# A two-block transformer with a 32-expert layer: the first and last expert written out, the first one's down weights beside the ring, the routing without GpSimd, and the gate's bias rows moved

## Chip, cores and metric

One NeuronCore of a Trainium2 chip. The metric is the device time of one execution in microseconds (us); the kernel before takes 2494.17 us, the median of three runs (2492.13 to 2497.22).

## What is computed

A sequence of 256 tokens of width 1024, all in fp32, goes through two layers of one kind (feed-forward, a mixing layer, cross attention, feed-forward) and then one layer of a second kind (a recurrence and a gated linear attention), which ends in a mixture of experts. The change lies in this last part:

```python
logits = xt @ w_router + b_router                  # 256 tokens, 32 experts
top_val, top_idx = lax.top_k(logits, 4); gates = softmax(top_val)
# for every expert e and the tokens that chose it:
hdn = xb @ w_up[e] + b_up[e]                       # 1024 -> 2048
gate_h = minimum(hdn[:, :1024], 7.0); up_h = clip(hdn[:, 1024:], -7.0, 7.0)
act = (up_h + 1.0) * gate_h * sigmoid(1.702 * gate_h)
y = (act @ w_down[e] + b_down[e]) * gate           # 1024 -> 1024, summed over the four experts
# then
h = layer_norm_2(DEEPNORM_ALPHA * h + m, ln2_g, ln2_b)
h = h + sigmoid(h @ w_ple_gate + b_ple_gate) * (p @ w_ple)
```

An expert's up weights are 8 MB and its down weights 4 MB; all 32 are read whatever the routing, 384 MB.

## The kernel before, in words

Every engine has its program written out by hand, with semaphores between them. A helper class counts the semaphores, so a wait names an event. SyncE issues all loads. Weights go through a ring of 12 slots of 1 MB (`ring`, slots 0 to 11). In front of the experts only slots 0 to 5 are filled in turn (`load`, L363); 6 to 11 hold split weights and inputs there. For the experts, `load_pair` (L375) fills two slots by one DMA of 2 MB: four pairs `("moe","u",k)` and two pairs `("moe","d",j)` are one expert, the whole ring. The first pair goes to slots 6 and 7. Each DMA waits until both of its slots are given back by TensorE (`used`), and stands in order behind the one before.

In front of the experts come the output projection (L1041), a layer norm over two halves of 128 tokens, t = 0 and 1 (`ln`, tag "A"), and the routing. For each half TensorE transposes the normed rows (`transposes`, L653), ScalarE copies half of the result to `hT` (L1368), VectorE the other (`evac_T`, L1850), and TensorE multiplies by the router weights (L1074, L1076). `best(t)` on VectorE (L2265 to L2273) takes the four highest and marks them in `chosen`. `best(0)` stands in `first_half`, which `ln` calls ahead of VectorE's copy for t = 1. GpSimd computes `h = hn * g + b` of both halves (`residual`, L2474 and L2475). From `chosen` TensorE counts each token's place in its expert (L1117), VectorE reads the largest count (`most`, L2299 to L2301), and every engine branches on it: at most 64 tokens to an expert is `few()`, else `many()`. The runs here take `few()`.

`few()` on TensorE: `expert_biases` multiplies the 32 gates of each token with the down biases (L1133, over 32 rows) and so opens the sums of banks 4 to 7. `gather` (L1157) picks an expert's tokens by a matmul with a selection matrix that VectorE wrote (`select`, L2322). Then a loop over 32 experts: `gate_up` (L1189, 64 matmuls that give back the eight up slots pair by pair), `turned(0)`, the next expert's `gather`, `turned(1)`, `combine("back")` (L1166) that adds the previous expert's result, the gates turned (`GT`), and the down matmuls (L1227). ScalarE copies out, takes the sigmoid (L1753) and copies the down result (L1338). After the loop stands `combine("last")`.

After the branch, VectorE adds the residual (`joined`, L2409) and norms (L2425), TensorE writes the gate's bias into banks 4 to 7 by matmuls over one row (`gate_bias(t)`, L1295, one ahead of and one behind the transposes of t = 0), transposes, and multiplies by `w_ple_gate` (L1302).

An fp32 matmul of the program shows as two records (MATMUL) in the trace.

## Time and profile before

| what | value |
|---|---|
| median of three runs | 2494.17 us |
| the profiled execution, its own time | 2496.79 us |
| its span, first to last instruction | 2495.0 us |
| PE, PEld busy | 2438.0 us (98%), 1792.1 us (72%) |
| DVE, ACT, POOL busy | 1106.1, 829.3, 201.0 us |
| read from HBM | 662.50 MB |

PE is TensorE's matmuls and PEld its weight loads, DVE VectorE, ACT ScalarE, POOL GpSimd, SP SyncE. A busy PE is not PE at its peak. The page cuts the span into 40 slices: up to slice 24 the DMA engines move 137 to 246 GB/s, in slices 26 to 39 they move 428 to 429. A row of the timeline has the start, the duration, engine, line, operation and tiles, and in brackets how long the engine had been idle before it and what ended that.

### The profile page before, as it was taken

What the parts mean: (1) busy time and instruction counts of PE and PEld (TensorE: products, weight loads), DVE (VectorE), ACT (ScalarE), POOL (GpSimd) and SP (SyncE); (2) the same over time, 40 slices, a digit from 0 to 9 for tenths busy, and PEclk for the clock granted to TensorE, in tenths of its full rate; (3) what the DMA queues carried; (4) which work ended last, traced back from release to release, by engine and by line L of the source; (5) the groups of instructions that cost most, each with busy time, mean ns of one, the idle gap of its engine ahead of it and who ended that gap; (6) DMA issues with size and microseconds to landing.
All of it is one profiled execution on the core that took longest, in us unless ns stands there. A gap on an engine that the chain in (4) does not pass through costs nothing. (4 is left out here: it accounts for less than half of the span.)

```text
span 2495.0 us, 36318 instructions
## 1 busy us (share of the span) xinstructions
PE 2438.0 (98%) x15029; PEld 1792.1 (72%) x15029; DVE 1106.1 (44%) x1439; ACT 829.3 (33%) x961; POOL 201.0 (8%) x96
## 2 busy tenths in 40 slices
PE   9999999999999999999999999999999999999998
PEld 8999988999999998899998954444444444444443
DVE  4557766644644867654568651221112121111123
ACT  4344344433433434433346411222112221211121
POOL 0002402200200340120020010000000000000000
PEclk9999999999999999999999998999999999999998
DMA  7665454565555545456545465999999999999992
GB/s 242 211 203 168 137 186 146 172 204 170 186 189 185 169 138 184 135 189 204 166 161 161 163 240 244 428 428 429 428 428 428 429 428 428 429 429 429 429 428 114
DMA packets 215595, 665.16 MB, mean 267 GB/s; under 512 B 9873, under 2 KB 164239, under 8 KB 190912
## 3 DMA queue, kind: packets, MB, share of 16 engines
q1 hardware_dynamic: 215488, 663.57, 69.9%
q8 instruction: 86, 1.41, 0.2%
q14 instruction: 21, 0.17, 0.0%
HBM read 662.50 MB, written 1.05 MB: 266 GB/s over the span
## 5 line engine op out<-in xcount | busy, mean ns | idle before, releaser
L607 PE MATMUL ps<-ring_halves 128*128 128x256 f32 x5984 | 754.2, 284 | 0.0
L607 PEld LDWEIGHTS ps<-ring_halves 128*128 128x128 f32 x5984 | 735.1, 192 | 3.6 <-issue 0.6
L1832 DVE TENSOR_TENSOR ring_halves<-ring,ring_halves 128x2048 fp32r<-128x2048 f32 x206 | 511.5, 2491 | 361.2 <-ACT ring_halves L1350 361.1
L1350 ACT CAST ring_halves<-ring 128x2048 fp32r<-128x2048 f32 x206 | 391.2, 1903 | 276.3 <-PE ps L607 141.7
L1189 PE MATMUL ps<-ring,work 128*64 128x512 f32 x2048 | 451.3, 595 | 22.8 <-DMA ring<-in_w_up_dram 22.1
L1338 ACT COPY work<-ps 128x512 f32<-128x512 f32 x190 | 109.7, 586 | 840.9 <-PE ps L1189 389.8
L1189 PEld LDWEIGHTS ps<-ring,work 128*64 128x64 f32 x2048 | 145.4, 137 | 322.7 <-issue 268.7
L2334 DVE TENSOR_SCALAR work<-work 128x128 f32<-128x128 f32 x64 | 19.3, 344 | 611.6 <-PE ps L1189 611.6
L618 PE MATMUL ps<-ring_halves,work_halves 128*128 128x512 f32 x1184 | 288.4, 391 | 0.0
L618 PEld LDWEIGHTS ps<-ring_halves,work_halves 128*128 128x128 f32 x1184 | 219.7, 188 | 44.4 <-issue 0.5
L1227 PE MATMUL ps<-ring,work 128*64 128x512 f32 x1024 | 226.8, 595 | 2.0
L1227 PEld LDWEIGHTS ps<-ring,work 128*64 128x64 f32 x1024 | 70.7, 137 | 137.5 <-issue 127.9
L2474 POOL TENSOR_TENSOR h<-hn,work 128x1024 f32<-128x1024 f32 x18 | 74.0, 4113 | 1117.2 <-DVE ring_halves L1858 1031.1
L618 PE MATMUL ps<-ring_halves 128*128 128x512 f32 x544 | 138.4, 393 | 1.3 <-ACT work L1338 1.3
L1157 PE MATMUL ps<-work,h 128*128 128x64 f32 x1056 | 133.0, 286 | 0.0
L1157 PEld LDWEIGHTS ps<-work,h 128*128 128x128 f32 x1056 | 130.0, 200 | 1.5 <-issue 1.5
L691 PE MATMUL ps<-hT,ring 128*128 128x128 f32 x1024 | 118.1, 276 | 3.4 <-ACT hT L1368 3.4
L691 PEld LDWEIGHTS ps<-hT,ring 128*128 128x128 f32 x1024 | 116.2, 192 | 6.6 <-ACT hT L1368 6.6
L618 PEld LDWEIGHTS ps<-ring_halves 128*128 128x128 f32 x544 | 101.6, 188 | 23.7 <-issue 2.9
L2351 DVE TENSOR_TENSOR work<-work 128x256 f32<-128x256 f32 x64 | 27.2, 426 | 135.6 <-ACT work L1753 131.7
L1406 ACT ACTIVATE work<-ps 128x512 f32<-128x512 f32 x44 | 26.3, 597 | 138.2 <-PE ps L607 138.2
L1166 PE MATMUL ps<-work 64*128 64x512 f32 x264 | 65.6, 615 | 0.7 <-ACT work L1338 0.7
(256 smaller groups left out, 1735.5 us busy)
## 6 DMA issues: line engine op xcount, KB each, us to landing
ring<-in_w_up_dram SPq DMA_DIRECT2D x128, 2048.0 KB, 23.7
ring<-in_w_down_dram SPq DMA_DIRECT2D x64, 2048.0 KB, 19.3
ring<-in_w_in_dram SPq DMA_DIRECT2D x52, 1024.0 KB, 5.2
ring<-in_ffn_gate_dram SPq DMA_DIRECT2D x44, 1024.0 KB, 5.3
ring<-in_ffn_up_dram SPq DMA_DIRECT2D x44, 1024.0 KB, 5.3
ring<-in_ffn_down_dram SPq DMA_DIRECT2D x44, 1024.0 KB, 4.9
ring<-in_w_out_dram SPq DMA_DIRECT2D x12, 1024.0 KB, 4.9
ring<-in_ca_k_dram SPq DMA_DIRECT2D x8, 1024.0 KB, 5.2
```

The source lines that it names most:

```text
L607: mm = pe.matmul(ps[:, bank, pt * T:pt * T + T], wt[:, o:o + P], x[:, k, :], start=(k == 0 and n == 0), stop=(k == DT - 1 and n == 2))
L618: mm = pe.matmul(ps[:, 4 + 2 * t + half, :], x, wt[:, o:o + 512], start=(start and n == 0), stop=(stop and n == 2))
L691: mm = pe.matmul(ps[:, bank, pt * T + t * P:pt * T + t * P + P], ring[:, slot_of[name], o:o + P], hT[:, k, t * P:t * P + P], start=(k == 0 ...
L1157: mm = pe.matmul(ps[:, 2, k * CAP:k * CAP + CAP], h[:, t, strip(("A",), k)], work[:, GS + t * CAP:GS + t * CAP + CAP], start=(t == 0), sto ...
L1166: mm = pe.matmul(ps[:, 4 + 2 * t + half, :], work[lo:lo + CAP, GGT + t * P:GGT + t * P + P], work[lo:lo + CAP, YS:YS + 512], start=False, ...
L1189: mm = pe.matmul(ps[lo:lo + CAP, x, :], work[:, XG + k * CAP:XG + k * CAP + CAP], ring[:, s, c0 + 512 * x:c0 + 512 * x + 512], start=(k == ...
L1227: mm = pe.matmul(ps[half * CAP:half * CAP + CAP, 3, :], work[:, ACTS + f * CAP:ACTS + f * CAP + CAP], ring[:, s, kk * D + half * 512:kk * ...
L1338: nc.scalar.copy(dst, ps[:, bank, :] if src is None else src).then_inc(emptied[bank].sem, 1)
L1350: nc.scalar.copy(high_of(name)[:], ring[:, s, :]).then_inc(hi_done.add(name), 1)
L1832: v.tensor_tensor(ring_halves[s][:], ring[:, s, :], high_of(name)[:].bitcast(F32), ALU.subtract)\
L2351: done(v.tensor_tensor(w(ACTS + 256 * x, 256), uh, w(SG + 256 * x, 256), ALU.mult), ("few", x))
L2474: link(g.tensor_tensor(h[:, t, :], hn[:, t, :], w(at, D), ALU.mult))
```

## The change

1. **Extra cells.** Four pieces of the work memory of 1 MB each (`EXTRA`, from offsets 11776, 13824, 1024 and 9728) take the first expert's down weights, by `load_extra`. SyncE writes the first expert out: its four up pairs, the down biases (now with a line of their own, `bias_in`), the two extra pairs, and then a loop over the other 31. So the second expert's first up pairs go to slots 2 to 5, where the first expert's down weights were.
2. **Experts written out.** On TensorE, VectorE and ScalarE `few()` is the first expert, a loop over 30, and the last. The first has no `combine("back")`, the last has no `gather` and no `select`. `many()` has its first expert written out.
3. **Routing.** `best(0)` moves behind `evac_T` of t = 1. GpSimd computes `h` of t = 0 alone; VectorE does t = 1 in two steps, the product behind `best(0)` and the sum behind the gates ("rows"). The two memsets that cleared `GGT` and `YS` go. `gather("xg0")` moves ahead of `expert_biases`. The turned gates go to bank 1.
4. **Bias rows.** The gate's bias matmuls go to banks 0 to 3 and stand at the end of each branch (`gate_biases`), all four together; the transposes behind the experts use banks 4 to 7.

```diff
-BDOWN, BUPROWS, ROUTER, BEFORE = R + 1024, TH + 1024, 20000, 20256
+BDOWN, BUPROWS, ROUTER, BEFORE = 5120, TH + 1024, 20000, 20256
+EXTRA = (XC, R, 1024, Y)
...
+            def load_extra(name, second, s, src):
+
+                loaded[s].add(name)
+                for x, i in ((name, s), (second, s + 1)):
+                    used[i].add(x)
+                    slot_of[x] = i
+                    sp.wait_ge(used[i].sem, used[i].at(x))
+                    plain(sp)
+                lo, step = EXTRA[s - RING], EXTRA[s - RING + 1] - EXTRA[s - RING]
+                dst = w(lo, 2 * step, "p (s n) -> p s n", s=2)[:, :, 0:SLOT]
+                sp.dma_start(dst, src.rearrange("p (s n) -> p s n", s=2)).then_inc(loaded[s].sem, 16)
...
             pos[0], size[0] = FIRST_PAIR, RING
-            with counted(book, sp, "e", EXPERTS, loaded + used) as e:
+            for k in range(0, DT, 2):
+                load_pair(weight("first", "u", k), weight("first", "u", k + 1), wup[:, 0, k // 2, :])
+            sp.wait_ge(dve_done.sem, dve_done.at(("y", "g", 3)))
+            sp.dma_start(work[0:32, BDOWN:BDOWN + 1024], a["b_down_2"].rearrange("a e n -> (a e) n"))\
+                .then_inc(bias_in.add("bdown"), 16)
+            load_extra(weight("first", "d", 0), weight("first", "d", 1), RING, wdn[:, 0, 0, :])
+            slot_used(sp, "w2o3")
+            load_extra(weight("first", "d", 2), weight("first", "d", 3), RING + 2, wdn[:, 0, 1, :])
+            with counted(book, sp, "e", EXPERTS - 1, loaded + used) as e:
...
             def few():
-                expert_biases("few")
                 pe.wait_ge(h_ready.sem, h_ready.at(("h", ("A",))))
+                pe.wait_ge(dve_done.sem, dve_done.at("rows"))
                 pe.wait_ge(sel_ready.sem, sel_ready.at("sel0"))
                 gather("xg0")
-                with counted(book, pe, "few", EXPERTS, emptied + [pe_full], "e") as e:
-                    def gate_up():
+                expert_biases("few")
...
+                def expert(ph):
+                    gate_up(ph)
+                    turned(ph, 0)
+                    if ph != "last":
+                        pe.wait_ge(sel_ready.sem, sel_ready.at((ph, "sel")))
+                        gather((ph, "xg"))
+                    turned(ph, 1)
+                    if ph != "first":
+                        combine((ph, "back"))
+                    gates_turned(ph)
+                    down(ph)
+
+                expert("first")
+                with counted(book, pe, "few", EXPERTS - 2, emptied + [pe_full], "e"):
+                    expert("next")
+                with last_expert():
+                    expert("last")
+                evacuated(3, ("last", "y"))
                 combine("last")
...
+            def gate_biases(branch):
+                row = arrived("bpg")
+                for b in range(4):
+                    open_bank(b, ("pg", branch))
+                    o = 512 * (b % 2)
+                    mm = pe.matmul(ps[:, b, :], ones[0:1, :], ring[0:1, row, o:o + 512], start=True, stop=False)
+                mm.then_inc(used[row].sem, 1)
...
             with pe.If(n < CAP + 1):
                 few()
-                fork.end("few", [1] * 4 + [0] * 5)
+                gate_biases("few")
+                fork.end("few", [0] * 9)
...
             def first_half():
                 dve.wait_ge(tables.sem, tables.at("all"))
-                v.memset(w(GGT, 256), 0.0)
-                done(v.memset(w(YS, 512), 0.0), "clear")
-                link(best(0))
 
             ln(("A",), ("ln1_g_2", "ln1_b_2"), 0, ALPHA2, first_half)
+            link(best(0))
+            mine(("hn", ("A",), 1))
+            dve.wait_ge(lnp_in.sem, lnp_in.at((("A",), 1)))
+            done(v.tensor_tensor(h[:, 1, :], hn[:, 1, :], w(LNP["A"], D), ALU.mult), "scaled")
             done(best(1), "chosen")
...
             done(ins, "gates")
+            mine("scaled")
+            done(v.tensor_tensor(h[:, 1, :], h[:, 1, :], w(LNP["A"] + D, D), ALU.add), "rows")
```

**VectorE's program, routing, before** (from the last op ahead of `best(0)`):

```order
L2281 MEMSET work 128x256
L2282 MEMSET work 128x512
L2265 COPY work<-ps 128x32
L2267 MAX work<-work 128x8
L2268 TENSOR_SCALAR small<-work 128x1
L2269 MAX_INDEX top_at<-work 128x8
L2270 CAST work<-top_at 128x8
L2271 TENSOR_SCALAR work<-work 128x32
L2273 SCALAR_TENSOR_TENSOR work<-work 128x32 x3
L1850 TENSOR_SCALAR hT<-ps,cols 128x128 x4
L2265 COPY work<-ps 128x32
```

**and now**, the same place (L2336 to L2344 is `best`, L1921 `evac_T`, L2357 the product of t = 1):

```order
L1921 TENSOR_SCALAR hT<-ps,cols 128x128 x4
L2336 COPY work<-ps 128x32
L2338 MAX work<-work 128x8
L2339 TENSOR_SCALAR small<-work 128x1
L2340 MAX_INDEX top_at<-work 128x8
L2341 CAST work<-top_at 128x8
L2342 TENSOR_SCALAR work<-work 128x32
L2344 SCALAR_TENSOR_TENSOR work<-work 128x32 x3
L2357 TENSOR_TENSOR h<-hn,work 128x1024
L2336 COPY work<-ps 128x32
```

The copy to `hT` (`128x128 x4`) has moved from behind `best(0)` to ahead of it, and a 128x1024 product stands between the two calls.

**VectorE's program behind the second `best`, now** (L2362 to L2367 make the gates, L2373 reads the largest count):

```order
L2362 TENSOR_TENSOR work<-work 128x64
L2363 TENSOR_REDUCE small<-work 128x2
L2364 RECIPROCAL small<-small 128x2
L2367 TENSOR_SCALAR work<-work,small 128x32 x2
L2370 TENSOR_TENSOR h<-h,work 128x1024
L2373 TENSOR_REDUCE small<-ps 128x1
```

The sum of t = 1 (L2370) has come in between the gates and the reading of the largest count.

**TensorE's program from the routing into the first expert, before** (L1133 the bias rows, L1157 the gather, L1189 gate and up):

```order
L1085 MATMUL ps<-work 128x512 x2
L1124 MATMUL ps<-ident,work 32x128 x2
L1280 TENSOR_LOAD most
L1281 COMPARE_AND_BRANCH
L1133 MATMUL ps<-work 128x512 x4
L1157 MATMUL ps<-work,h 128x64 x16
L120 UNCONDITIONAL_BRANCH
L120 ISA
L582 REGISTER_ALU
L1184 REGISTER_ALU
L589 ISA
L1189 MATMUL ps<-ring,work 64x512 x24
```

**and now** (L1170 the bias rows, L1194 the gather, L1229 gate and up, L1242 and L1251 transposes):

```order
L1153 MATMUL ps<-work 128x32
L1121 MATMUL ps<-work 128x512 x2
L1160 MATMUL ps<-ident,work 32x128 x2
L1349 TENSOR_LOAD most
L1350 COMPARE_AND_BRANCH
L1194 MATMUL ps<-work,h 128x64 x16
L1170 MATMUL ps<-work 128x512 x4
L1229 MATMUL ps<-ring,work 64x512 x32
L1242 MATMUL ps<-ident,work 128x128 x4
L1194 MATMUL ps<-work,h 128x64 x16
L1242 MATMUL ps<-ident,work 128x128 x4
L1251 MATMUL ps<-ident,work 128x128 x2
```

The gather stands ahead of the bias rows, and the first expert is written out ahead of the loop.

**TensorE's program at the end of the experts, before** (L1166 `combine`, L1227 down, L1281 the jump over `many()`, L1295 the gate's bias rows, L1302 the gate):

```order
L1227 MATMUL ps<-ring,work 64x512 x8
L1222 REGISTER_ALU
L1227 MATMUL ps<-ring,work 64x512 x8
L120 REGISTER_ALU
L120 COMPARE_AND_BRANCH
L1166 MATMUL ps<-work 128x512 x4
L1281 UNCONDITIONAL_BRANCH
...
L1295 MATMUL ps<-ring,ones 128x512 x2
L653 MATMUL ps<-ident,hn 128x128 x8
L1295 MATMUL ps<-ring,ones 128x512 x2
L1302 MATMUL ps<-ring,hT 128x512 x8
```

**and now** (L1203 `combine`, L1251 the gates turned, L1264 down, L1343 the bias rows, L1350 the jump, L1365 the gate):

```order
L1203 MATMUL ps<-work 128x512 x4
L1251 MATMUL ps<-ident,work 128x128 x2
L1264 MATMUL ps<-ring,work 64x512 x16
L1203 MATMUL ps<-work 128x512 x4
L1343 MATMUL ps<-ring,ones 128x512 x4
L1350 UNCONDITIONAL_BRANCH
...
L689 MATMUL ps<-ident,hn 128x128 x8
L1365 MATMUL ps<-ring,hT 128x512 x8
```

All bias rows stand ahead of the jump, and nothing but the transposes is left between the jump and the gate's matmuls.

## Rows read from the trace of the kernel before

**Rows 1.** Busy time by stretch, expert stage; `PEclk` 1.00 is TensorE at full clock.

```profile
core 0: us, PE busy (x) PEld busy (x) DVE busy (x) ACT busy (x) POOL busy (x), PEclk, DMA share, GB/s
1494.00:1520.57 26.57, 25.36 (x77) 14.53 (x78) 2.36 (x12) 4.44 (x8) 0.00 (x0) 0.61 0.00 1
...
1520.57:1541.84 21.27, 21.21 (x116) 10.24 (x114) 5.36 (x16) 4.13 (x7) 0.00 (x0) 1.00 0.95 394
...
1717.51:1745.64 28.13, 28.07 (x148) 12.54 (x146) 5.35 (x16) 6.00 (x9) 0.00 (x0) 1.00 1.01 429
...
2200.00:2229.35 29.35, 28.27 (x148) 12.47 (x146) 5.36 (x16) 5.98 (x10) 0.00 (x0) 1.00 1.01 429
```

**Rows 2.** Timeline of SyncE's queue: weight loads issued around the first experts.

```profile
1468.90 8.15 SPq L375 DMA_DIRECT2D ring<-in_w_down_dram  x2
...
1520.57 10.62 SPq L375 DMA_DIRECT2D ring<-in_w_up_dram  x4
...
1541.84 3.77 SPq L375 DMA_DIRECT2D ring<-in_w_down_dram  x2
...
1548.71 10.61 SPq L375 DMA_DIRECT2D ring<-in_w_up_dram  x4
```

**Rows 3.** Timeline, routing: second half of the tokens turned, then routed.

```profile
1480.88 2.37 POOL L2474 TENSOR_TENSOR h<-hn,work 128x1024 f32<-128x1024 f32 x1 [6.32 <-DVE hn L1872]
...
1480.92 1.11 PE L653 MATMUL ps<-ident,hn 128*128 128x128 f32 x8
...
1483.31 2.39 DVE L2271 TENSOR_SCALAR work<-work 128x32 f32<-128x32 f32 x1
...
1486.60 1.37 DVE L1850 TENSOR_SCALAR hT<-ps,cols 128x128 f32<-128x128 f32 x4
...
1488.07 0.60 PE L1074 MATMUL ps<-brout,ones 1*128 1x32 f32 x2 [4.32 <-DVE hT L1850]
```

**Rows 4.** Timeline: choice for the second half, to the first expert.

```profile
1492.26 0.19 DVE L2265 COPY work<-ps 128x32 f32<-128x32 f32 x1 [4.29 <-PE ps L1076]
...
1494.41 0.22 DVE L2290 TENSOR_TENSOR work<-work 128x64 f32<-128x64 f32 x1
...
1499.79 0.54 DVE L2322 TENSOR_SCALAR work<-work 128x64 f32<-128x64 f32 x2 [0.73 <-DVE work L2301]
...
1502.35 5.04 PE L1133 MATMUL ps<-work 32*128 32x512 f32 x8 [0.45 <-ACT work L1738]
...
1507.32 7.09 PE L1157 MATMUL ps<-work,h 128*128 128x64 f32 x32
...
1515.17 7.29 PE L1189 MATMUL ps<-ring,work 128*64 128x512 f32 x26 [0.76 <-ACT work L1338]
```

**Rows 5.** Granted clock in the middle of the bias rows.

```profile
1504.00:1505.00 1.00, 1.00 (x3) 0.52 (x2) 0.00 (x0) 0.00 (x0) 0.00 (x0) 0.78 0.00 0
```

**Rows 6.** Timeline of the last expert.

```profile
2425.99 3.65 PE L1189 MATMUL ps<-ring,work 128*64 128x512 f32 x16 [1.00 <-DMA ring<-in_w_up_dram]
...
2430.15 3.93 PE L1157 MATMUL ps<-work,h 128*128 128x64 f32 x32
...
2436.95 7.09 PE L1227 MATMUL ps<-ring,work 128*64 128x512 f32 x32
```

**Rows 7.** Timeline after the last expert, to the gate's matmuls.

```profile
2444.72 1.99 PE L1166 MATMUL ps<-work 64*128 64x512 f32 x8 [0.68 <-ACT work L1338]
...
2450.59 1.00 DVE L2425 TENSOR_SCALAR hn<-hn,mv,rstd 128x512 f32<-128x512 f32 x2
...
2450.72 3.75 PE L1295 MATMUL ps<-ring,ones 1*128 1x512 f32 x4 [4.01 <-issue]
...
2454.39 1.97 PE L653 MATMUL ps<-ident,hn 128*128 128x128 f32 x8
...
2460.00 8.96 PE L1302 MATMUL ps<-ring,hT 128*128 128x512 f32 x16
...
2471.15 1.22 DVE L2441 TENSOR_TENSOR h<-hn,work 128x1024 f32<-128x1024 f32 x1
```

More of the change, by code:

```diff
@@ L573, in _ @@
         def _(pe):
-            for s in range(RING):
+            for s in range(RING + len(EXTRA)):
                 pe.sem_inc(used[s].sem, 1)
@@ new lines, in turned, with gates_turned @@
+                def turned(ph, x):
+                    pe.wait_ge(emptied[x].sem, emptied[x].at((ph, "gu", x), 1))
+                    emptied[x].add((ph, "gut", x))
+                    for f in range(4):
+                        mm = pe.transpose(ps[:, x, f * P:f * P + P],
+                                          work[:, bass.ds(GUT + 512 * x + f, P, step=4)], ident[:])
+                    full(mm, (ph, "gut", x))
+                def gates_turned(ph):
+                    open_bank(2, (ph, "GT"))
+                    if ph == "last":
+                        pe.wait_ge(dve_done.sem, dve_done.at("last gates"))
@@ L1269, in many @@
+                expert("first")
+                with counted(book, pe, "many", EXPERTS - 1, emptied + [pe_full], "e"):
+                    expert("next")
                 for t in range(TT):
@@ L1756, in few @@
+                    pe_group((ph, "GT"))
                     nc.scalar.copy(w(GGT, 256), ps[:, 2, 0:256]).then_inc(emptied[2].sem, 1)
-                    slot_used(act, ("moe", "d", 3))
+                    slot_used(act, weight(ph, "d", 3))
                     copy_out(3, w(YS, 512))
+                expert("first")
+                with counted(book, act, "few", EXPERTS - 2, [act_done], "e"):
+                    expert("next")
+                with last_expert():
+                    expert("last")
@@ L1768, in _ @@
+                expert("first")
+                with counted(book, act, "many", EXPERTS - 1, [act_done], "e"):
+                    expert("next")
             act.wait_ge(dve_done.sem, dve_done.at("most"))
```

308 lines of the change are left out of this document (158 added, 150 removed).

## The prediction, made before the changed kernel ran

> **What bounds it now.** I read the windows first. Up to the experts TensorE is the bound. In the expert stage two limits take turns. TensorE needs 28.13 us for an expert when all its weights are there: it is busy 28.07 of it, at full clock [rows 1], and SyncE's first up load of one expert follows that of the one before after 28.14 us (1520.57 and 1548.71) [rows 2]. The loads of an expert are 12.58 million bytes, at 429 GB/s [rows 1] 29.3 us. So TensorE is the faster by 1.2 us an expert; it lives on a lead of one full ring at first, and later waits for the last up pair [rows 6]. From then on the loads set the pace. What sets the start of the stage's end is then the last moment at which the loads had nothing to do.
>
> The issue rows show that moment. The ring is full by about 1494: from there to 1520.57 the loads move 1 GB/s [rows 1]. At 1520.57 the first expert's first up pair is given back and the loads restart; call this R. The eight up slots come back faster than they are filled (8.39 million bytes, 19.6 us), and the down slots come back at 1541.84, 21.27 us after R, so there is one more short idle time (share 0.95, 394 GB/s in that stretch) [rows 1, 2]. From 1541.84 on the loads never rest. The last up pair is there at 2425.99 [rows 6], 905.4 us after R.
>
> So three things can move the end: R itself, the idle time of the loads just behind R, and what stands behind the last up pair.
>
> **Routing (moves R).** What the timeline shows is TensorE idle for 4.32 us, waiting for VectorE's copy of the transposed rows (L1850) at 1486.60, which stands behind `best(0)` [rows 3]. In that call one 128x32 operation took 2.39 us while GpSimd's 128x1024 product and sum ran. Now the copy comes first. The transposes end at 1480.92 + 1.11 = 1482.03, the copy at 1483.4. Router(1) can follow at about 1483.8; at half clock it took 4.2 (1488.07 to 1492.26) [rows 3, 4], at full half of that. `best` without GpSimd beside it takes 2.15 us (1492.26 to 1494.41) [rows 4]: `best(0)` to 1485.6, the product of t = 1 (1.22, as the same shape in [rows 7]) to 1486.9, `best(1)` to 1489.1 (0.9 more if router(1) ran at half clock); before, that was 1494.41. Five small operations for the gates, 0.22 each as L2290 [rows 4], and the sum, 1.22, bring 1491.4; TensorE counts places meanwhile. Three small reads (0.7 with their links), the branch (0.73) and `select` (0.54) [rows 4] follow, so select ends at about 1493.6 where it ended at 1500.33.
>
> Before, TensorE then had bias rows and gather in a row, and the first gate-and-up matmul started at 1515.17, R being 5.40 us later. Now it is gather, bias rows, gate-up; the copy of the gather (0.76 with its wait, [rows 4]) hides beside the bias rows. The price of these depends on the clock. The gather takes 3.93 at 2.4 GHz and 7.09 at 1.2 [rows 4, 6]. The bias rows took 5.04 with the clock falling 2.2 us after their start (0.78 in the second from 1504) [rows 5]: 3.6 at full, 7.2 at half. A first pair of gate-up is 3.65 at full [rows 6], 7.3 at half, 5.40 as it was. All at full: R = 1493.7 + 3.93 + 3.6 + 3.65 = 1504.9, 15.7 us earlier. All at half: 1515.3, 5.3 earlier. I take the middle: the clock stays up through the routing, since its one long idle time is gone, and falls at the small work as it did in the middle of the bias rows; gather 3.93, bias rows 7.2, pair 5.40. R = 1510.2: **10.3 us** earlier. The two memsets that go stood ahead of `best(0)`; nothing waits for them now either, so they count nothing.
>
> **Extra cells.** The first two extra pairs and the second expert's first two up pairs are 8.39 million bytes. They start where the down loads did (the last of those was issued at about 1477, [rows 2]), and are in by about 1494, ahead of R. So at R the loads have 4.19 million bytes fewer to do, 9.8 us. Most of that is lost again: at R only four up slots and the down slots of the second expert are to be filled, 19.6 us, and the next slot comes back when TensorE has used the second expert's first pair, 28.13 after R. The loads idle there for 8.5 us, and once more in front of that expert's down slots, at R + 28.13 + 21.27. From there they never rest, with one expert less to go. The end of that chain is R + 28.13 + 905.4 - 29.3 = R + 904.2: **1.2 us** gained, not 9.8. That the down biases now come behind the first up pairs costs nothing: they are in by about 1472 and read after 1497.
>
> **Last expert.** Behind the last up pair (3.65) TensorE gathers for an expert that does not exist, 3.93 us [rows 6]. It goes. The down weights are 4.9 and 9.8 us behind the last up pair, at 2430.9 and 2435.8; the down matmuls would start at 2433.5 in place of 2436.95 and need the second pair 3.5 later, at 2437. So 3.4 us are gained, 0.5 short of the gather, since the transposes, `combine` and the turned gates remain and the copies between them are no longer covered.
>
> **Bias rows and jump.** `combine` ends 3.4 us earlier, at 2443.3. Before, TensorE then stood idle for 4.01 us [rows 7], during which nothing but the end of the branch lies; no wait of VectorE explains it. Then came bias rows at half clock (3.75), the transposes (1.97), bias rows again (about 3.7), and the gate's matmuls at 2460.00. Now the bias rows (3.6) follow `combine` at once. They give no signal, so the branch's own waits need not wait for them, and the 4.01 runs beside them, to 2447.3. VectorE's normed rows are there at 2451.59 - 3.4 = 2448.2, half of them 0.5 earlier. Transposes to 2449.7, copies to 2451.3 at half clock, then the gate: 8.7 us earlier than 2460.00. Of its first matmuls 16 records took 8.96 [rows 7] where 0.45 each, as a bias record at full clock, is 7.2: 1.8 were lost to half clock. Now it may be a little more, I take 0.7. Sum with the last expert: **8.0 us**. If the 4.01 only starts behind the bias rows, it is 5.6; if the clock stays up, 11.
>
> **Sum.** 10.3 + 1.2 + 8.0 = 19.5 us. The profiled execution took 2496.79, 2.6 over the median; its successor would take 2477.3, and the median 2494.17 - 19.5 = **2474.7 us**. About 0.2%, 5 us, is what a measurement of this kernel can tell from no change.
>
> **Rivals.**
> - *The clock stays up from the routing to the first expert.* For: the 4.32 us idle time ahead of the fall is gone. Against: in the old trace it fell in bias rows that had hardly a gap before them [rows 5]. R is 15.7 earlier: 2469.3. (The Trainium skill, page TensorE: Matmul & The Clock Gate, Part 1, ties the clock to how busy the engine was; by that rule, read as idle time alone, this rival would be the forecast.)
> - *Half clock all the way, and the jump not hidden.* For: 0.61 on average from 1494 to R [rows 1], and the new stretch has the same small matmuls. 5.3 + 1.2 + 5.6 = 12.1: 2482.1.
> - *The extra cells count in full,* 9.8 in place of 1.2, if TensorE's pace did not hold back the slots. Against: the 28.13. 2466.1.
> - *A loop that stalls (slower).* The programs are longer, and TensorE's loop lies elsewhere in its program. The jump at the end of the branch went with 4.01 us of idle time [rows 7]. If each of 29 jumps back cost that, an expert would take 32.1, TensorE would be the bound, and the last pair would come at 1510.2 + 31 x 28.13 + 29 x 4.01 + 7.3 = 2505.8, 79.8 late: 2566. From 1.5 us a jump on, nothing is gained. Against: the old loop holds as much per turn and is busy 28.07 of 28.13. (The Trainium skill, page Runtime: NRT & Kernel Launch, section Instruction fetch mechanics, says that a taken branch outside the pages held makes the engine fetch first; the old loop shows none of it, the jump over `many()` may.)
>
> **Chances.** Forecast 0.56, clock up 0.18, half clock 0.17, cells in full 0.04, stall 0.04, anything else that leaves it within 0.2%, 0.01. The forecast's own range is 2470 to 2480 (R between the two clock cases, tail 5.6 to 11). The range reaches to the clock cases with the runs' spread of 2 us: 2466 to 2484. Faster 0.94, same 0.02, slower 0.04.
>
> **What will show it.** Router(1) right behind the embedding matmuls with no idle time, select about 6.7 us earlier, R near 1510; the idle time of the loads 8.5 us long behind the first expert and a short one 21 us later; 28.13 an expert early and 29.3 late; R to the last up pair 904.2; no gather in the last expert; the gate's matmuls 10 us after the start of the last `combine`, where they were 15.3. It is wrong if the loads are still idle after the third expert's down slots, if the pair of R comes later than 1515, or if an expert takes TensorE over 29.3.

## The result, and the profile after

Beside each other on one chip, the changed kernel took 2477.38 us (median of 5 runs, 2474.97 to 2483.20) and the kernel before 2494.61 (5 runs, 2492.13 to 2497.22). The ratio is 0.9934, 95% interval 0.9917 to 0.9950. The forecast was 2474.7 within 2466 to 2484; the median lies 2.7 us above it. The profiled execution of the changed kernel is its fastest, 2474.97 with a span of 2473.2, and the profiled one before (span 2495.0) is among the slower of its kind. So the two traces differ by 21.8 us, the medians by 17.2.

The head of the page after, and its two queues of instruction packets (q8 carries TensorE's, q14 VectorE's):

```profile
span 2473.2 us, 36110 instructions
...
PE 2414.8 (98%) x14989; PEld 1778.6 (72%) x14989; DVE 1104.3 (45%) x1437; ACT 748.4 (30%) x897; POOL 196.3 (8%) x94
...
q8 instruction: 88, 1.44, 0.2%
q14 instruction: 22, 0.18, 0.0%
```

That q8 is TensorE's and q14 VectorE's is my reading, from when their packets come beside those engines' stalls; no row says it.

Lines of the program have moved: the transposes L653 are now L689, the router L1074 is L1110, the places L1117 are L1153, the gather L1157 is L1194, the first bias rows L1133 are L1170, gate-and-up L1189 is L1229, down L1227 is L1264, `combine` L1166 is L1203, the gate's bias L1295 is L1343, its matmuls L1302 are L1365, and `joined` is L2503.

The same windows as [rows 1], cut at the new give-backs:

```profile
core 0: us, PE busy (x) PEld busy (x) DVE busy (x) ACT busy (x) POOL busy (x), PEclk, DMA share, GB/s
1476.00:1502.85 26.85, 25.37 (x133) 15.69 (x134) 11.96 (x43) 7.55 (x16) 0.00 (x0) 1.00 0.58 235
1502.85:1532.69 29.84, 27.81 (x142) 12.48 (x140) 5.35 (x16) 4.72 (x8) 0.00 (x0) 0.94 0.69 282
1532.69:1553.80 21.11, 21.11 (x116) 10.44 (x114) 5.36 (x16) 2.86 (x6) 0.00 (x0) 1.00 0.96 396
...
1616.69:1644.69 28.00, 28.00 (x150) 12.54 (x148) 5.35 (x16) 3.45 (x7) 0.00 (x0) 1.00 1.00 428
2200.00:2229.36 29.36, 28.21 (x148) 12.44 (x146) 5.35 (x16) 3.45 (x7) 0.00 (x0) 1.00 1.01 429
```

The pattern is the forecast one. The loads have idle time behind the first expert (share 0.69, 282 GB/s), a little more 21 us after the second expert's first give-back (0.96), and none from 1553.80 on. TensorE's pace is 28.00 early, the loads' pace is 29.36 late. Early it was 28.13. ScalarE's program per expert is shorter by two table loads now (ACT busy 6.00 in 28.13 before, 3.45 in 28.00 now); whether the 0.13 us come from that is not shown.

SyncE's queue, where [rows 2] showed 1520.57, 1541.84 and 1548.71:

```profile
1476.17 30.76 SPq L391 DMA_DIRECT2D ring<-in_w_up_dram  x4
...
1502.85 4.08 SPq L391 DMA_DIRECT2D ring<-in_w_up_dram  x2
...
1509.68 3.76 SPq L391 DMA_DIRECT2D ring<-in_w_down_dram  x2
1532.69 10.70 SPq L391 DMA_DIRECT2D ring<-in_w_up_dram  x4
...
1553.80 3.76 SPq L391 DMA_DIRECT2D ring<-in_w_down_dram  x2
```

The first row merges all four up pairs of the second expert; the second row, from a view of a later window, is the last two of these four. So two pairs are issued from 1476.17 on, ahead of time, and the third waits for the first give-back. That is R = 1502.85.

The routing, from the transposes of t = 1 to the first expert; its rows of before are [rows 3, 4]:

```profile
1479.30 1.11 PE L689 MATMUL ps<-ident,hn 128*128 128x128 f32 x8
...
1480.52 1.37 DVE L1921 TENSOR_SCALAR hT<-ps,cols 128x128 f32<-128x128 f32 x4 [1.34 <-PE ps L689]
...
1482.10 0.38 PE L1110 MATMUL ps<-brout,ones 1*128 1x32 f32 x2
...
1490.62 0.54 DVE L2398 TENSOR_SCALAR work<-work 128x64 f32<-128x64 f32 x2 [0.73 <-DVE work L2375]
...
1491.40 3.95 PE L1194 MATMUL ps<-work,h 128*128 128x64 f32 x32 [0.76 <-DVE work L2398]
1495.29 3.70 PE L1170 MATMUL ps<-work 32*128 32x512 f32 x8
...
1498.91 13.95 PE L1229 MATMUL ps<-ring,work 128*64 128x512 f32 x64
```

The work ahead of the experts varies by some us between executions, so I measure from T1, the start of these transposes (1480.92 before, 1479.30 after). The copy no longer waits, the router (L1110) follows at once, select stands at T1 + 11.3 in place of T1 + 18.9, and gather and bias rows run at 2.4 GHz. R is T1 + 23.55, where it was T1 + 39.65.

What follows in the first expert had no row before:

```profile
1517.90 1.28 ACT L1816 ACT_TABLE_LOAD   x1
1517.94 0.44 PE L1251 MATMUL ps<-ident,work 128*128 128x128 f32 x2 [0.16 <-ACT work L1399]
1519.20 0.42 ACT L1816 ACTIVATE work<-work 128x256 f32<-128x256 f32 x1
...
1520.24 8.74 PE L1264 MATMUL ps<-work 128*64 128x512 f32 x32 [1.87 <-issue]
```

The first expert has no result of an earlier one to combine. Nothing covers ScalarE's table load and sigmoid, so TensorE stands idle for 1.87 us ahead of the down matmuls; and these take 8.74 us in place of 7.09, since the clock falls to half in them (PEclk 0.94 over the expert).

Last expert and tail, where [rows 6, 7] stood:

```profile
2408.18 3.65 PE L1229 MATMUL ps<-ring,work 128*64 128x512 f32 x16 [1.15 <-DMA ring<-in_w_up_dram]
...
2415.48 7.09 PE L1264 MATMUL ps<-ring,work 128*64 128x512 f32 x32
2423.25 1.99 PE L1203 MATMUL ps<-work 64*128 64x512 f32 x8 [0.69 <-ACT work L1399]
2425.17 4.28 PE L1343 MATMUL ps<-ring,ones 1*128 1x512 f32 x8
...
2430.13 1.28 DVE L2503 SCALAR_TENSOR_TENSOR hn<-h,ps 128x512 f32<-128x512 f32 x2 [13.01 <-issue]
...
2434.80 1.94 PE L689 MATMUL ps<-ident,hn 128*128 128x128 f32 x8 [5.35 <-DVE hn L2519]
2438.34 7.12 PE L1365 MATMUL ps<-ring,hT 128*128 128x512 f32 x12 [1.60 <-ACT hT L1429]
```

The chain of waits has one long piece here that is no work (first line below), and for the stretch from 2423.3 to 2430.2 the DMA view lists packets of instructions:

```profile
2425.36 4.78 issue
```

```profile
q8 instruction: 2, 0.03, 2.0%
q14 instruction: 2, 0.02, 0.6%
```

From the last `combine` to the gate's matmuls it is 15.09 us; it was 15.28. The bias rows did move under the jump, but VectorE's first addition, `joined(0)`, comes 6.88 us after `combine`'s start where it came 1.89 us after it. The stretch was to shrink by 5 us, and shrank by 0.2.

The whole, in us, between the profiled executions (spans):

| stretch | before | after | gain |
|---|---|---|---|
| start to T1 | 1480.92 | 1479.30 | 1.6 (varies by run) |
| T1 to R | 39.65 | 23.55 | 16.1 |
| R to the last up pair | 905.42 | 905.33 | 0.1 |
| last up pair to the last `combine` | 18.73 | 15.07 | 3.7 |
| to the gate's first matmul | 15.28 | 15.09 | 0.2 |
| to the end | 35.00 | 34.86 | 0.1 |

### The profile page after: what moved, and what is told of

It reads as the page before. It is cut to its first block and busy times, and to the rows that moved or that the text cites. A ratio compares the mean times of both kernels' runs of the same rounds, so it can differ in the third digit from the quotient of the medians.

```text
span 2473.2 us, 36110 instructions
## 1 busy us (share of the span) xinstructions
PE 2414.8 (98%) x14989; PEld 1778.6 (72%) x14989; DVE 1104.3 (45%) x1437; ACT 748.4 (30%) x897; POOL 196.3 (8%) x94
## 5 line engine op out<-in xcount | busy, mean ns | idle before, releaser
L1229 PE MATMUL ps<-ring,work 128*64 128x512 f32 x2048 | 449.8, 593 | 24.3 <-DMA ring<-in_w_up_dram 24.3
L1229 PEld LDWEIGHTS ps<-ring,work 128*64 128x64 f32 x2048 | 145.6, 137 | 323.2 <-issue 267.4
L1264 PE MATMUL ps<-ring,work 128*64 128x512 f32 x992 | 219.7, 595 | 0.0
L1264 PEld LDWEIGHTS ps<-ring,work 128*64 128x64 f32 x992 | 68.7, 137 | 129.0 <-issue 123.9
L1194 PE MATMUL ps<-work,h 128*128 128x64 f32 x1024 | 125.8, 281 | 0.8 <-DVE work L2398 0.8
L1194 PEld LDWEIGHTS ps<-work,h 128*128 128x128 f32 x1024 | 123.1, 196 | 1.0 <-issue 1.0
L1203 PE MATMUL ps<-work 64*128 64x512 f32 x256 | 63.6, 615 | 0.7 <-ACT work L1399 0.7
```

Source lines behind the costliest of these rows:

```text
L1194: mm = pe.matmul(ps[:, 2, k * CAP:k * CAP + CAP], h[:, t, strip(("A",), k)], work[:, GS + t * CAP:GS + t * CAP + CAP], start=(t == 0), sto ...
L1203: mm = pe.matmul(ps[:, 4 + 2 * t + half, :], work[lo:lo + CAP, GGT + t * P:GGT + t * P + P], work[lo:lo + CAP, YS:YS + 512], start=False, ...
L1229: mm = pe.matmul(ps[lo:lo + CAP, x, :], work[:, XG + k * CAP:XG + k * CAP + CAP], cell(s)[:, c0 + 512 * x:c0 + 512 * x + 512], start=(k == ...
L1264: mm = pe.matmul(ps[half * CAP:half * CAP + CAP, 3, :], work[:, ACTS + f * CAP:ACTS + f * CAP + CAP], cell(s)[:, kk * D + half * 512:kk * ...
```

## Experiments

Each kernel is the changed one with the edit shown. Ratios are to the kernel before, run in turn on the same chip. Its median was 2492.2 in the first four experiments, 2494.1 in the next four, 2492.4 in the next three and 2493.7 in the last. The changed kernel's own interval is 0.9917 to 0.9950, and by the times only routing_back (9) and all_three (11) lie clear of it. What the other experiments show is read from their traces, one execution each.

**1. Is it the jump over `many()`?** (no_many)

```
             def many():
-                expert_biases("many")
-                ...
+                pass
```

> The changed kernel with the body of many() left out on TensorE, VectorE and ScalarE (a branch that the data here never take, so the work done is the same). Theory 'the jump over many() makes an engine fetch its program': VectorE's first operation behind the branch, which came 5.8 us after the end of the last combine's first half in the changed kernel, comes 1 us after it, as in the kernel before; the page's --dma view by window shows no or fewer instruction packets there; about 4 to 5 us faster than the changed kernel. Rival 'VectorE waits for a semaphore there': no change.

Measured: 2473.87 (2470.76 to 2477.3), ratio 0.9923 (0.9908 to 0.9939).

```profile
2427.66 1.99 PE L1203 MATMUL ps<-work 64*128 64x512 f32 x8 [0.68 <-ACT work L1354]
2429.03 1.29 DVE L2404 SCALAR_TENSOR_TENSOR hn<-h,ps 128x512 f32<-128x512 f32 x2 [7.51 <-PE ps L1203]
...
2437.25 8.67 PE L1320 MATMUL ps<-ring,hT 128*128 128x512 f32 x16 [1.59 <-ACT hT L1384]
```

The body of `many()` is left out on TensorE, VectorE and ScalarE. With nothing to jump over, `joined(0)` follows `combine` after 1.37 us, with no packet of instructions between the two starts, and the gate follows after 9.59 us. 5.5 us of the tail hang on the jump in this pair of traces. The times show less, 2.7 us by the two ratios: R came later here, at T1 + 25.2.

**2. The same without losing the branch** (tail_in_branch). VectorE's first rows and TensorE's first transposes and 16 gate matmuls are written into both branches, ahead of the jump.

```
                 gate_biases("few")
                 fork.end("few", [0] * 9)
+                fork.tail(gate_opened)
 ...
                 few()
                 fork.end("few", [0])
+                fork.tail(normed_rows)
```

> The changed kernel with VectorE's rows behind the experts (joined, statistics, rows, the first copy) and TensorE's first transposes and 16 gate records written into each branch, ahead of the jump over many(). Theory 'fetch behind the jump': VectorE starts 1 us after the combine's first half, TensorE's gate matmuls start 4 to 5 us earlier than in the changed kernel, the fetch is hidden: 4 to 5 us faster than it. Rival 'VectorE waits for something else': no change.

Measured: 2473.29 (2471.72 to 2475.32), ratio 0.9918 (0.9904 to 0.9932). `joined(0)` comes 1.32 us after `combine`, the gate's matmuls 9.50 us after it. By the ratios that is 4.0 us faster than the changed kernel, with R at T1 + 28.6. Code that needs the branch's result at once belongs ahead of the jump.

**3. Are the extra cells worth anything?** (no_extra)

```
-            load_extra(weight("first", "d", 0), weight("first", "d", 1), RING, wdn[:, 0, 0, :])
-            slot_used(sp, "w2o3")
-            load_extra(weight("first", "d", 2), weight("first", "d", 3), RING + 2, wdn[:, 0, 1, :])
+            load_pair(weight("first", "d", 0), weight("first", "d", 1), wdn[:, 0, 0, :])
+            load_pair(weight("first", "d", 2), weight("first", "d", 3), wdn[:, 0, 1, :])
```

> The changed kernel without the extra cells: the first expert's down weights go to ring slots 2 to 5, all else the same. Theory 'the first slots come back at TensorE's pace, so most of the 4 MB is lost': from the first give-back (R) to the last up pair 906 to 907.5 us, where the changed kernel has 905.3; 1 to 2 us slower than it. Rival 'the cells count in full': 9.8 us slower.

Measured: 2480.87 (2478.75 to 2481.68), ratio 0.9948 (0.9933 to 0.9963). R is T1 + 28.58 here, since the clock fell in the bias rows. From R to the last up pair it is 906.0, against 905.3. So the four cells gave 0.7 us in this pair of traces, although the first expert took 1.65 us longer in the changed kernel's. Against wide_bias (10), which has the cells and the same 28.19 us for the first expert as here, it is 1.9. This stretch moves by some 2 us between executions (see the end), so the size isn't settled; the rival's 9.8 isn't there. The difference in time is not clear of noise, and the 5.0 us of R, the clock's, would account for it.

**4. Is it the place of `best(0)`?** (choice_early)

```
+                link(best(0))

             ln(("A",), ("ln1_g_2", "ln1_b_2"), 0, ALPHA2, first_half)
-            link(best(0))
```

> The changed kernel with best(0) back ahead of VectorE's copy of t = 1; VectorE still does the rows of t = 1. Theory 'TensorE's idle time at that place costs itself and then the clock': an idle time of TensorE of about 2.5 us (best(0) without GpSimd beside it), R 1 to 3 us later if the clock stays at 2.4 GHz, 8 to 11 us later if it falls. Rival 'the clock falls in small matmuls, whatever the idle time': no more than 2.5 us.

Measured: 2480.15 (2476.09 to 2480.68), ratio 0.9944 (0.9928 to 0.9959). The copy for t = 1, and the router behind it:

```profile
1483.79 1.36 DVE L1921 TENSOR_SCALAR hT<-ps,cols 128x128 f32<-128x128 f32 x4
...
1485.25 0.37 PE L1110 MATMUL ps<-brout,ones 1*128 1x32 f32 x2 [0.59 <-DVE hT L1921]
```

TensorE waits 0.59 us, not the 2.5 expected, in place of 4.32 before [rows 3]. The gather starts at T1 + 12.14, as in the changed kernel (12.10). The order alone is worth nothing.

**5. Is it GpSimd beside `best`?** (pool_rows)

```
-                for t in range(1 if tag[0] == "A" else TT):
+                for t in range(TT):
 ...
-            done(v.tensor_tensor(h[:, 1, :], hn[:, 1, :], w(LNP["A"], D), ALU.mult), "scaled")
-            done(v.tensor_tensor(h[:, 1, :], h[:, 1, :], w(LNP["A"] + D, D), ALU.add), "rows")
```

> The changed kernel with the rows of t = 1 back on GpSimd (product and sum), best(0) staying behind VectorE's copy. Theory 'GpSimd's operations made best(0) slow': one or two small operations of best(0) take 1 to 2.4 us again, the gather for the first expert starts 2 to 4 us later than the 12.1 us behind the start of t = 1's transposes that the changed kernel shows. Rival 'the order of best(0) was the cause': 12 us or less, since VectorE has 2.4 us less to do.

Measured: 2480.23 (2478.73 to 2483.59), ratio 0.9945 (0.9928 to 0.9961). The expected delay in the routing did not come.

```profile
1484.85 2.34 POOL L2560 TENSOR_TENSOR h<-h,work 128x1024 f32<-128x1024 f32 x1
...
1485.75 1.47 DVE L2338 CAST work<-top_at 128x8 f32<-128x8 uint32 x1
```

One of VectorE's small operations still takes 1.47 us beside GpSimd, where it takes 0.17 without; it ends 0.03 us after GpSimd's operation. But VectorE has the long product and the long sum less, and the gather starts at T1 + 11.41, 0.7 us *earlier* than in the changed kernel.

**6. Is it the order of bias rows and gather?** (bias_first)

```
+                expert_biases("few")
                 pe.wait_ge(h_ready.sem, h_ready.at(("h", ("A",))))
                 ...
                 gather("xg0")
-                expert_biases("few")
```

> The changed kernel with the bias rows back ahead of the first gather. Theory: the bias rows wait for ScalarE's copy of the turned gates but not for select; select is done 1 us later, so most of their 3.7 us is paid either way, and the copy of the gather (0.7 us) is uncovered: first gate-and-up matmul 0 to 1 us later. Rival 'the order was what gained': 3 us or more later. The clock may fall in the bias rows in either; the comparison is by the starts, not by the whole time.

Measured: 2480.57 (2478.89 to 2482.57), ratio 0.9947 (0.9931 to 0.9964). The bias rows take 3.70 us in front, the clock falls right behind them, and the gather takes 7.01 us at half clock; the copy of its result costs 0.88 us of idle time. R is T1 + 30.15, 6.6 us later than in the trace of the changed kernel and 1.6 later than in the trace of no_extra, where the clock also fell early. Even these 1.6 are in part the clock's, which was at half all through the gather here. At full clock I estimate, from the gather's start at T1 + 15.4, 3.95 for it, 0.88 idle and 3.94 for the first pair: R at T1 + 24.2, so the order alone is worth some 0.6 us, as expected, and up to 6.6 with what the clock happens to do.

**7. The gate's bias rows put back** (old_bias)

```
-                gate_biases("few")
-                fork.end("few", [0] * 9)
+                fork.end("few", [1] * 4 + [0] * 5)
 ...
+            gate_bias(0)
             transposes(last, 0, hn)
+            gate_bias(1).then_inc(used[row].sem, 1)
```

> The changed kernel with the gate's bias rows back behind the branch, two ahead of and two behind the transposes, in banks 4 to 7. Theory 'VectorE's fetch behind the jump now sets the start of the gate': TensorE's bias rows ahead of the transposes are hidden behind it, those behind them cost about 3.7 us at half clock less 1.6 us that TensorE waits for the copies anyway: 2 us slower than the changed kernel. Rival 'the bias rows are what gained': 5 us or more slower.

Measured: 2481.63 (2480.48 to 2483.87), ratio 0.9953 (0.9937 to 0.9970). From `combine` to the gate it is 17.51 us, against 15.09: the move of the bias rows is worth 2.4 us as long as VectorE is late anyway.

**8. The tail of experiment 2, and the table loaded early** (tail_and_table)

```
+                nc.scalar.activation(small[:, 62:63], epsc[:, 0:1], ACT.Sigmoid)
                 pe_group("xg0")
                 copy_out(2, w(XG, 512))
```

> tail_in_branch with one small sigmoid on ScalarE ahead of the first expert, so that the table load does not stand between the first expert's gate-and-up and down matmuls. Theory 'TensorE waited 1.87 us there for the table load': that idle time shrinks to about 0.6, the first expert takes 28 to 28.6 us where it took 29.8, 1.3 us faster than tail_in_branch. Rival 'it is program fetch': the idle time stays.

Measured: 2468.99 (2468.81 to 2473.79), ratio 0.9908 (0.9891 to 0.9924).

```profile
1521.06 4.51 PE L1278 MATMUL ps<-work 128*64 128x512 f32 x20 [0.46 <-issue]
```

TensorE's idle time ahead of the first expert's down matmuls is 0.46 in place of 1.87, the first expert takes 26.78 us in place of 28.18 in tail_in_branch, and from R to the last up pair it is 903.0. That is 3.1 less than in tail_in_branch: more than the 1.4 of the idle time. The rest is in when the loads land, which differed by as much between traces of code that is the same there (see the end). This version is clearly faster than the kernel before. Against the changed kernel all its runs are lower, but the intervals of the ratios overlap.

**9. All three parts of the routing put back together** (routing_back: the edits of 4, 5 and 6 in one; the two memsets stay out and the turned gates stay in bank 1)

> The changed kernel with all three parts of its routing put back at once: GpSimd does both tiles' rows again, best(0) stands ahead of the copy L2338 again, and the bias rows stand ahead of the gather. Each alone left the time from the start of t=1's transposes (T1) to the gather's start at 11.4 to 12.2 us (bias_first: 15.4, the 3.7 of its bias rows in it). My theory: the long idle time of TensorE (4.32 us in the kernel before) needs both, best(0) ahead of the copy and GpSimd's rows that slow it down; so here TensorE is idle for some 4 us after t=0's router, the clock falls to half after that, the gather starts at T1 + 25 to 27, the first up pair comes back at T1 + 39 to 40 against T1 + 23.5, and the time is 10 to 16 us above the changed kernel's 2477.4, at 2485 to 2494. Rival: the parts add up, each is worth only what it cost alone (0 to 3 us), then the gather starts at about T1 + 16, and the time is 2480 to 2484.

Measured: 2490.71 (2486.56 to 2496.02, 10 runs), ratio 0.9989 (0.9980 to 0.9999).

```profile
1481.82 2.39 DVE L2339 TENSOR_SCALAR work<-work 128x32 f32<-128x32 f32 x1
...
1486.57 0.60 PE L1108 MATMUL ps<-brout,ones 1*128 1x32 f32 x2 [4.32 <-DVE hT L1918]
...
1500.84 5.06 PE L1168 MATMUL ps<-work 32*128 32x512 f32 x8 [0.45 <-ACT work L1796]
1505.83 7.09 PE L1192 MATMUL ps<-work,h 128*128 128x64 f32 x32
```

These are the rows of before [rows 3, 4], to the hundredth where it matters: 2.39 beside GpSimd, 4.32 idle, then half clock and 7.09 for the gather. R is T1 + 39.70. The median is 13.3 us above the changed kernel's (by the two ratios 13.7), of 17.2 gained in all. Not all of it need be the routing's. Between the two traces it is 19.1 us: 16.1 in the routing, 2.4 between R and the last up pair, the rest ahead of T1 and in the tail. The routing's share cannot be split among its edits: two of them alone cost nothing that shows ahead of the gather and the third 0.6 to 6.6, all three 16.1. The idle time needs `best(0)` ahead of the copy *and* GpSimd beside it; either edit removes it.

**10. Does the narrow matmul let the clock fall?** (wide_bias)

```
-                        mm = pe.matmul(ps[:, 4 + 2 * t + half, :], work[0:32, GT + t * P:GT + t * P + P],
-                                       work[0:32, BDOWN + half * 512:BDOWN + half * 512 + 512], start=True, stop=True)
+                        mm = pe.matmul(ps[:, 4 + 2 * t + half, :], work[:, GT + t * P:GT + t * P + P],
+                                       work[:, BDOWN + half * 512:BDOWN + half * 512 + 512], start=True, stop=True)
 ...
+            v.memset(w(GT, T), 0.0)
             link(best(0))
```

> The changed kernel, with the eight matmuls of the first bias rows (L1170) over all 128 rows of the array in place of 32: the 96 further rows of the gates are set to zero ahead of them (one more VectorE instruction, some 0.1 to 0.3 us, off TensorE's path), so that the product is the same. In the nine kernels traced the clock fell to half in or after these rows in eight. If matmuls over 32 rows are what lets it fall there, it now stays at 2.4 GHz from T1 to the first expert's down matmuls, the bias rows take 3.7 us, gate-up starts at T1 + 19.6, the first up pair comes back at T1 + 23.5 in every execution, the times lie closer together (within 4 us), and the median is 2 to 5 us below the changed kernel's. Rival: what counts is the idle time and the narrow matmuls of the router and of the transposes ahead of it; then the clock falls all the same, in one place or another, and the median is that of the changed kernel, 2475 to 2481.

Measured: 2472.62 (2472.55 to 2476.32), ratio 0.9920 (0.9906 to 0.9934). First the windows of wide_bias, then of tail_in_branch, whose TensorE code there differs by the width alone; both are cut at the bias rows' start and at R:

```profile
1494.14:1501.65 7.51, 7.51 (x30) 2.75 (x31) 0.00 (x0) 0.58 (x1) 0.00 (x0) 1.00 0.01 2
1501.65:1529.84 28.19, 26.16 (x142) 12.55 (x140) 5.35 (x16) 4.72 (x8) 0.00 (x0) 1.00 0.73 298
```

```profile
1495.00:1508.02 13.02, 13.02 (x33) 4.33 (x33) 0.00 (x0) 0.59 (x1) 0.00 (x0) 0.61 0.00 1
1508.02:1536.20 28.18, 26.15 (x141) 12.46 (x139) 5.35 (x16) 4.72 (x8) 0.00 (x0) 1.00 0.73 299
```

TensorE is busy throughout in both first rows. Over 32 rows the clock is at 0.61 on average in this trace and the stretch takes 13 us; over 128 rows it is 1.00 and takes 7.5. tail_in_branch is, with no_extra, the slowest case over 32 rows. The changed kernel's own trace is the fastest, at 1.00 through this stretch, and R did not move against it: R is T1 + 23.64 here, the clock also stays up through the first expert's down matmuls behind the same 1.87 us of idle time, and the runs lie within 3.8 us where those of the changed kernel spread over 8.2. The medians of the two differ by 4.8 us, but the intervals of their ratios overlap. So the gain isn't shown by the times; what the traces show is that R, T1 + 25.2 to 28.6 in seven others over 32 rows, is at T1 + 23.6 in both over 128.

**11. All of it** (all_three: the edits of 2, 8 and 10)

> tail_and_table (2469.0, the rows of the tail written in both branches, and the sigmoid's table loaded early) with the bias rows over 128 rows as in wide_bias as well. If the 128 rows keep the clock up, 2466 to 2469, with the gate's matmuls 9.5 us after the last combine's start and the first up pair back at T1 + 23.5. Rival: no difference to tail_and_table, 2469 to 2473.

Measured: 2467.94 (2465.37 to 2470.45), ratio 0.9898 (0.9883 to 0.9913). PEclk is 1.00 from T1 to the second expert, R is T1 + 23.63, from R to the last up pair it is 902.5, and the gate comes 9.21 us after `combine`. It is the fastest kernel of the study; against the changed kernel (0.9917 to 0.9950) the intervals are apart, against tail_and_table (0.9891 to 0.9924) they overlap.

**12. The last expert back in the loop** (last_in_loop)

```
-                with counted(book, pe, "few", EXPERTS - 2, emptied + [pe_full], "e"):
+                with counted(book, pe, "few", EXPERTS - 1, emptied + [pe_full], "e"):
                     expert("next")
-                with last_expert():
-                    expert("last")
```

> The changed kernel with the last expert back in the loop (31 passes in place of 30 and one written out): it gathers once more for an expert that isn't there, and its gates are turned behind its first combine again. The changed kernel's last expert takes 7.30 us from the start of its last up pair's 16 matmuls to the start of its down matmuls, where the kernel before takes 10.96. My theory: here it takes 10.8 to 11.0 again, the last combine starts 18.7 us behind the last up pair in place of 15.07, the first give-back of the first expert and the distance from it to the last up pair (905.3) stay as they are, and the time is 3.7 us above the changed kernel's for the same clock, 2479 to 2485. Rival: less code stands in the branch, so the instruction fetch ahead of VectorE's joined(0), 6.88 us behind the last combine's start, is over sooner and gives part of it back: joined(0) starts 2 to 4 us behind the combine and the time is 2476 to 2479.

Measured: 2475.39 (2474.63 to 2477.38), ratio 0.9924 (0.9908 to 0.9941): not slower at all.

```profile
2410.76 3.65 PE L1229 MATMUL ps<-ring,work 128*64 128x512 f32 x16 [1.14 <-DMA ring<-in_w_up_dram]
...
2429.36 1.99 PE L1203 MATMUL ps<-work 64*128 64x512 f32 x8 [0.68 <-ACT work L1397]
...
2431.22 1.28 DVE L2497 SCALAR_TENSOR_TENSOR hn<-h,ps 128x512 f32<-128x512 f32 x2 [8.63 <-DVEq L151]
...
2439.01 9.19 PE L1363 MATMUL ps<-ring,hT 128*128 128x512 f32 x16 [1.59 <-ACT hT L1427]
```

Both theories are right in kind, each for its part, and the rival by more than it said; the time that mine gave is wrong. `combine` starts 18.60 us behind the last up pair (15.07 in the changed kernel), and that pair is 907.6 us behind R, where 905.3 was expected (see the end). But `joined(0)` follows it after 1.86 us in place of 6.88, and the gate after 9.65 in place of 15.09. One packet of q14 lands there between `combine`'s start and 2431.22, where the changed kernel has two. In this pair of traces, writing the last expert out gains 3.5 us ahead of `combine` and costs 5.4 between `combine` and the gate. That the length of the program is what does it is my reading; the runs show only that the stall is gone with that code.

## Why the prediction was right, and where not

The mechanisms were mostly right, but the close number is luck. The largest term was 5.8 us too small in the trace, the cells 1.1 and the tail with the last expert 4.1 too large, and they offset each other.

**Routing: mechanism right, the middle taken between the bounds too low.** Forecast 10.3 us, measured 16.1 in the trace, which is the rival "the clock stays up" (15.7) for this term. Select ended at T1 + 11.9, where I wrote T1 + 12.7 (my steps, added up, give 12.3 to 12.5). The step that failed is the clock's: I let it fall at the start of the bias rows (7.2 us) and in the first pair (5.40), and they took 3.70 and 3.94. That is 5.0 us of the 5.8; the earlier select is the rest. But that rival isn't the whole truth either: in seven other traces with this order of gather and bias rows, over 32 rows, and GpSimd idle, R lay at T1 + 25.2 to 25.3 (four times), 26.9, 28.6 and 28.6, a gain of 11 to 14.4. My middle value lies just below what these show, and the profiled execution above all of them. (The Trainium skill, page TensorE: Matmul & The Clock Gate, Part 1, ties the clock to how busy the engine was. For the old 4.32 us of idle time the trace agrees, since half clock followed it in routing_back. In the bias rows it doesn't: TensorE was busy throughout, and half clock came in or right behind them in 11 of 12 traces over 32 rows and in neither of two over 128.)

**Cause of the old idle time: right, but not separable.** I put the 4.32 us down to `best(0)` ahead of the copy, with one operation slowed by GpSimd. Experiments 4, 5 and 9 show that both are needed. It was two operations, and each ended with GpSimd's:

```profile
1482.28 0.99 DVE L2270 CAST work<-top_at 128x8 f32<-128x8 uint32 x1
...
1483.33 2.34 POOL L2475 TENSOR_TENSOR h<-h,work 128x1024 f32<-128x1024 f32 x1
```

The cast ends at 1483.27, 0.02 us after GpSimd's product [rows 3], and the operation of 2.39 us at 1485.70, 0.03 after this sum. So GpSimd's end set the time of the copy, which is why routing_back, without the memsets, shows the same 4.32.

**Extra cells: right that they don't count in full; their size is not settled.** 1.2 forecast, 0.1 measured. The argument (TensorE's pace holds back the slots) holds: the loads move the 8.4 MB of four pairs in 29.84 us, so at 429 GB/s they idle for some 10.2 us behind the first expert, where I had 8.5. The term missed 1.7 us in the first expert, 29.84 where I used 28.13: no row of before shows an expert without `combine`, and there the sigmoid and its table load are bare (1.87), and the clock falls. By my chain the gain is 29.3 less the first expert's time: -0.5 at 29.84, 1.1 at 28.19, 2.5 at 26.78. The traces show 0.1 (the changed kernel), 1.3 (wide_bias) and 2.4 and 2.9 (tail_and_table and all_three, where R to the last up pair is 903.0 and 902.5). But four others with 28.2 us for the first expert (no_many, tail_in_branch, choice_early, bias_first) have 905.9 to 906.1 and so gained nothing; their loads land late, as told at the end.

**Last expert: right.** 3.4 forecast, 3.7 measured. What I didn't have was its price elsewhere.

**Tail: the wrong step.** "VectorE's normed rows are there at 2451.59 - 3.4 = 2448.2" took VectorE's start, 1.9 us after `combine`, as given. I named the jump as a suspect for TensorE, and hid TensorE's 4.01 us under the bias rows. That worked: in last_in_loop TensorE jumps as well, and its gate matmuls wait for no more than VectorE's rows. But VectorE jumps over its own `many()` too, and its program had grown. `joined(0)` was 5.0 us late, and the gate came 15.1 us after `combine` and not 10. Of the 8.0 us for tail and last expert together, 3.9 came. With that stall gone (experiments 1, 2, 8, 11, 12) the gate came 9.2 to 9.7 us after `combine`, so the rest of that sum stood.

**Rivals.** The stalling loop did not happen: 28.00 us a turn, less than before. A stall at a jump did, once, at the end of the branch. (The Trainium skill, page Runtime: NRT & Kernel Launch, section Instruction fetch mechanics, says that a taken branch outside the pages held makes the engine wait for a fetch; the packets and the 4.78 us of "issue" agree, and experiments 1 and 2 show that the stall hangs on the jump; that the packets are what VectorE waited for is inferred.) "Half clock all the way" and "cells in full" did not happen either.

## What to carry to other kernels

Ask of every engine, not only of the bound one, what it must do first behind a jump, and put that work ahead of the jump in each branch: here it was worth 5.5 us in the traces, more than writing out the last expert (3.7). When parts of an edit each seem worth nothing undone alone, undo them together before calling them useless. A gain that ends at the granted clock needs several executions: one trace here showed 16.1 us where others with the same routing showed 11 to 14.

## What the runs showed of the hardware

- **Width and the clock.** Eight matmuls of 512 columns over 32 rows, with TensorE busy throughout, stand in 12 traces. In 11 of them the clock fell to half in these rows or within 0.6 us of their end; in the changed kernel's own it did not. Over 128 rows it stayed up there in both traces. So the width is the likely cause, on two traces; the same was tried nowhere else. It cost up to 5 us of R. Apart from that, the clock fell in the first expert's down matmuls in 5 of the 12, the changed kernel's among them, behind the 1.87 us of idle time.
- **What a jump costs varies.** In ten traces VectorE jumps over `many()` ahead of `joined(0)`. It came 6.1 to 7.3 us behind `combine` in eight of them and 1.9 in two, last_in_loop and the kernel before. In the four others (nothing to jump over, or the work ahead of the jump) it was 1.3 to 1.4. last_in_loop differs from the changed kernel by one expert's code. Which length is bad, or whether it is the length, I can't say; no run varied it alone.
- **VectorE beside GpSimd.** Small operations of 0.17 to 0.24 us took 0.99 to 2.39 us beside GpSimd's 128x1024 operations (before, routing_back, pool_rows), and each ended 0.02 to 0.04 us after GpSimd's operation did. Most of their neighbours kept their time.
- **When a load lands.** From the give-back of the second expert's down slots to the last up pair it took 854.4 us in the changed kernel, 854.8 in wide_bias, but 856.6 in last_in_loop and 856.7 in routing_back. It isn't the rate: from 1760 to 2360 the changed kernel and no_many both move 428 to 429 GB/s. The first pair issued behind the loads' last idle time landed 7.6 to 7.9 us after its issue in six traces (the kernel before, the changed one, no_extra, tail_and_table, wide_bias, all_three) and 9.8 to 10.2 us in the eight others, and the later pairs, where I compared them (the changed kernel and no_many), stayed about 2 us apart. What makes that pair late stays open.
